# A two-layer transformer block in fp32 parts: the layer loop written out, its barrier removed, the last norm by sums per token

## The reference, cut to what matters

```python
for l in range(DEPTH):                      # DEPTH = 2, D_MODEL = 1024, SEQ = 512
    h = rmsnorm(x, norm_mix[l])
    proj = h @ w_in[l]                      # 1824 columns, split into the mixers' inputs
    ...                                     # convolution, two attentions, pooling
    x = x + jnp.concatenate([ya, yb, yc, yd], axis=-1) @ w_out[l]
    x = x + memory_cross_attention(rmsnorm(x, norm_xa[l]), mem, mem_norm[l], ...)
    x = x + conv_glu_ffn(rmsnorm(x, norm_ffn[l]), ffn_up[l], ffn_dw[l], ffn_dw_b[l], ffn_down[l])
return rmsnorm(x, norm_final)
```

## Time and profile before

| | before |
|---|---|
| median of 3 runs | 1663.12 us (1661.73 to 1664.53) |
| the profiled execution | 1663.39 us |
| its span, first to last instruction | 1661.4 us |
| TensorE busy | 1581.5 us, 95% |
| VectorE, ScalarE, GpSimd busy | 1037.2, 718.8, 188.4 us |
| mean granted TensorE clock | 0.983 of full |
| DMA | 153.44 MB, 92 GB/s, 28.4% of 16 engines on the main queue |

### The profile page before, as it was taken

How to read it: one execution, slowest core, us unless ns; L and a number is a source line. 1 busy time by engine, 2 the same in 40 slices (tenths; PEclk the granted TensorE clock), 3 DMA queues, 4 the chain that set the end, 5 groups by cost and what they waited for, 6 DMA issues and landing times. The chain is left out here.

```text
span 1661.4 us, 21870 instructions
## 1 busy us (share of the span) xinstructions
PE 1581.5 (95%) x7784; PEld 1230.0 (74%) x7784; DVE 1037.2 (62%) x1579; ACT 718.8 (43%) x1114; POOL 188.4 (11%) x133
## 2 busy tenths in 40 slices
PE   5699999999899999999979999999999999999995
PEld 1287677688688888888868767778768888888874
DVE  7659976543456746745756997654344773674676
ACT  8722477442435423423442257653244442342343
POOL 0005014230030000000020501422003000000002
PEclk9899999999999999999989999999999999999998
DMA  4242233132032323232224223312302323233223
GB/s 161 88 155 89 74 117 103 39 101 89 13 101 90 95 95 101 89 101 93 84 83 144 88 77 118 99 49 100 94 13 89 102 88 102 91 98 96 94 83 107
DMA packets 45441, 153.44 MB, mean 92 GB/s; under 512 B 5040, under 2 KB 5296, under 8 KB 44464
## 3 DMA queue, kind: packets, MB, share of 16 engines
q1 hardware_dynamic: 45360, 152.33, 28.4%
HBM read 144.97 MB, written 7.34 MB: 92 GB/s over the span
## 5 line engine op out<-in xcount | busy, mean ns | idle before, releaser
L705 ACT ACTIVATE wh<-raw 128x1024 fp32r<-128x1024 f32 x228 | 241.4, 1059 | 609.6 <-PE psum L1329 599.4
L1326 PE MATMUL psum<-a_hi,wh 128*128 128x512 f32 x1072 | 422.6, 394 | 3.7 <-DVE wl L978 3.7
L1329 PE MATMUL psum<-a_hi,wl 128*128 128x512 f32 x1072 | 419.9, 392 | 0.0
L1328 PE MATMUL psum<-a_lo,wh 128*128 128x512 f32 x1072 | 419.9, 392 | 0.0
L978 DVE TENSOR_TENSOR wl<-raw,wh 128x1024 fp32r<-128x1024 f32 x224 | 276.9, 1237 | 147.7 <-ACT wh L705 147.5
L1326 PE MATMUL psum<-b_hi,wh 128*128 128x512 f32 x608 | 241.1, 397 | 8.2 <-DVE x_sb L1210 4.4
L1326 PEld LDWEIGHTS psum<-a_hi,wh 128*128 128x128 f32 x1072 | 203.2, 190 | 46.2 <-DVE wl L978 4.3
L1328 PE MATMUL psum<-b_lo,wh 128*128 128x512 f32 x608 | 237.4, 390 | 0.0
L1329 PE MATMUL psum<-b_hi,wl 128*128 128x512 f32 x608 | 237.3, 390 | 0.0
L1329 PEld LDWEIGHTS psum<-a_hi,wl 128*128 128x128 f32 x1072 | 202.9, 189 | 42.8
L1328 PEld LDWEIGHTS psum<-a_lo,wh 128*128 128x128 f32 x1072 | 203.3, 190 | 41.9
(11 more groups left out here) (208 smaller groups left out, 1933.8 us busy)
## 6 DMA issues: line engine op xcount, KB each, us to landing
raw<-in_w_main SPq DMA_DIRECT2D x106, 512.0 KB, 3.5
raw<-in_w_up SPq DMA_DIRECT2D x88, 512.0 KB, 3.5
raw<-in_w_down SPq DMA_DIRECT2D x32, 512.0 KB, 3.5
raw<-in_w_last SPq DMA_DIRECT2D x16, 384.0 KB, 3.0
bias_scratch<-stage SPq DMA_DIRECT2D x16, 256.0 KB, 2.0
bias<-bias_scratch SPq DMA_DIRECT2D x16, 256.0 KB, 3.8
raw<-in_w_first SPq DMA_DIRECT2D x6, 512.0 KB, 3.5
sw<-in_small SPq DMA_DIRECT2D x2, 1152.0 KB, 8.2
```

The lines of the kernel that those rows point to most:

```text
L705: act.activation(wh[:, b].rearrange("p k m -> p (k m)")[:, 0:width], raw[:, b, 0:width], ACT.Copy).then_inc(w_hi, 1)
L1326: pe.matmul(out_ap, wh[:, b, k, :], his[:, k, :], start=((begin or first) and i == 0), stop=False)
L1328: pe.matmul(out_ap, wh[:, b, k, :], los[:, k, :], start=False, stop=False)
L1329: last = pe.matmul(out_ap, wl[:, b, k, :], his[:, k, :], start=False, stop=(end and i == len(tiles) - 1))
```

## The change

The loop over layers becomes Python code: a function layer_program(layer) returns five engine programs, which one single block runs one behind the other, layer 0 and then layer 1. Each layer has its own set of 59 semaphores; those that both share count on. There is no barrier and no clearing of semaphores between the layers or ahead of the last norm. Since 123 is odd, chunk n of layer 1 uses the other half and the other bank (function slot).

At the end of layer 0's feed-forward, ACT and VectorE split the first two weight chunks of layer 1 (hi_of_next, lo_of_next), where in earlier steps they split chunks n + 2. TensorE begins layer 1 with chunk 0, waiting for each tile of a_lo, then the sums, then chunk 1 with the row in its middle. SyncE issues the loads of the first two chunks of layer 1 under the same conditions as before, and the layer's vectors once all low parts of x are there.

In the last layer a_hi and a_lo are not made after the feed-forward. GpSimd sums the squares of 7 tiles, and TensorE takes the eighth straight from sqx: sixteen recorded one-column matmuls. The last norm is then done as the others, by a 128x4 corner and row_of, and the scalings read the row from PSUM. ACT runs a one-column square root (L971) ahead of the last eight chunks, which puts the table load there.

```diff
-        with nc.Fori(0, L) as layer:
-            with nc.Block() as block:
+        def layer_program(layer):
+            own, prev = layer_sems[layer], layer_sems[layer - 1] if layer else None
...
+            def slot(b):
+                return (b + layer * N_END) % 2
...
+                if prev:
+                    for b in range(2):
+                        sp.wait_ge(prev.w_lo, N_END - 1 + b)
+                        sp.dma_start(raw[:, slot(b), :], w_first[layer, b]).then_inc(w_load[b], 16)
+                    sp.wait_ge(prev.x_lo, 3 * KT)
                 sp.dma_start(vec[:], vecs[layer]).then_inc(vec_in, 16)
...
-                    for b in (1, 0):
-                        sp.wait_ge(w_lo, N_END - b)
-                        sp.dma_start(raw[:, b, :], w_first[layer + 1, b]).then_inc(w_load[b], 16)
-                    for b in range(2):
-                        sp.wait_ge(w_load[b], ((N_END + 1 - b) // 2) * 16)
...
+                if not prev:
                     hi(0)
                     hi(1)
                 roots("stat_mix", c("eps6"), 1.0 / D)
                 row_of("stat_mix")
                 hi(2)
...
+                if last_layer:
+                    act.activation(xneg[:, 0:1], c("ones"), ACT.Sqrt)
                 for i in range(KT):
                     n = N_END - KT + i
                     if i < KT - 2:
                         hi(n + 2)
+                    elif not last_layer:
+                        hi_of_next(i - KT + 2)
                     act.wait_ge(g_dve, g_dve_count(n, "down"))
-                    split_x(i, 2, v("g_next", i))
+                    split_x(i, 2, None if last_layer else v("g_next", i))
...
                 for i in range(KT):
                     n = N_END - KT + i
                     residual(i, n)
                     if i < KT - 2:
                         lo(n + 2)
+                    elif not last_layer and i == KT - 2:
+                        lo_of_next(0)
+                    if not last_layer:
                         split_x(i, 2, v("g_next", i))
+                if not last_layer:
+                    lo_of_next(1)
...
+                if prev:
+                    pe.wait_ge(prev.g_freed_by_dve, g_dve_count(N_END - 2, "down"))
+                    gemm(0, 0, a_hi, a_lo, ready=lambda i: pe.wait_ge(prev.x_lo, 2 * KT + i + 1))
+                    pe.wait_ge(prev.x_squares_summed, 3 * KT)
+                    sums_of("stat_mix", (ssum, one))
+                    pe.wait_ge(prev.g_freed_by_dve, g_dve_count(N_END - 1, "down"))
+                    gemm(1, 1, a_hi, a_lo, tiles=range(4), end=False)
+                    row_of("stat_mix")
+                    gemm(1, 1, a_hi, a_lo, tiles=range(4, KT), begin=False)
+                else:
                     sums_of("stat_mix", (ssum, one))
                     gemm(0, 0, a_hi, a_lo)
                     row_of("stat_mix")
                     gemm(1, 1, a_hi, a_lo)
...
-            nc.all_engine_barrier(sems_to_clear=all_sems)
+                if last_layer:
+                    pe.wait_ge(ss_in, 3 * KT - 1)
+                    pe.wait_ge(sq_in, 3 * KT)
+                    sums_of("stat_out", (ssum, one), (sqx[:, 1, :], one))
+                    row_of("stat_out")
...
-                pe.matmul(V[0], ones, ssum[:], start=True, stop=True).then_inc(v_full, 1)
...
+                act.activation(thin[:, OUT, 0:4], V[V_BANK["stat_out"]][:, 0:4], ACT.Sqrt, bias=c("eps6"),
+                               scale=1.0 / D).then_inc(of_last.root_of_stat, 1)
...
+                dve.reciprocal(thin[:, OUT, 0:4], thin[:, OUT, 0:4]).then_inc(of_last.root_inverted, 1)
+                dve.wait_ge(of_last.v_full, V_AT["stat_out_row"] + 1)
                 for k in range(KT):
-                    dve.scalar_tensor_tensor(x_sb[:, k, :], x_sb[:, k, :], v("g_next", k), rbc[:],
+                    dve.scalar_tensor_tensor(x_sb[:, k, :], x_sb[:, k, :], v("g_next", k), V[V_BANK["stat_out_row"]],
                                              ALU.mult, ALU.mult).then_inc(x_up, 1)
```

More of the change, by code:

```diff
@@ L13 @@
+from collections import namedtuple
 from contextlib import ExitStack
@@ new lines, in vector @@
+                PAIR_STEPS = 3
+                for g in range(GROUPS + 1):
+                    tiles, base, f0 = GROUP_TILES[g], N_UP + g * N_GROUP, g * GROUP
+                    up_pair(base, 0, f0, first=(g == 0), tail=False)
+                    before = step.n
+                    with dve.Fori(1, tiles) as j:
+                        step.enter((j - 1) * PAIR_STEPS + before)
+                        up_pair(j * 2 + base, j, j + f0)
+                        step.leave(PAIR_STEPS, tiles - 1)
+                    out_lo(tiles - 1, f0 + tiles - 1)
+                    if g < GROUPS:
+                        n = base + 2 * tiles
+                        for s in range(2):
+                            residual(s, n + s)
+                            lo(n + s + 2)
+                        with dve.Fori(1, KT // 2) as j:
+                            for s in range(2):
+                                residual(j * 2 + s, j * 2 + n + s, (N_UP + s) % 2)
+                                lo(j * 2 + n + s + 2, (N_UP + s) % 2)
@@ L1633, in block_program @@
[L1633 to L1654 removed]
+                gemms(0, 9, a_hi, a_lo, S, "in", lead=2)
@@ new lines, in tensor @@
+                for i in range(2):
+                    ps = bank(f"vm{i}")
+                    for t in range(2):
+                        kb = 2 * i + t
+                        last = pe.matmul(ps[:, GW * t:GW * t + GW], ckv[:, kb * P:kb * P + P], sw[:, SW_V:SW_V + GW],
+                                         start=True, stop=True)
+                    last.then_inc(v_full, 1)
+                gemm(12, 0, a_hi, a_lo, free="in")
+                gemm(13, 1, a_hi, a_lo, free="in")
+                gemm(14, 0, a_hi, a_lo, free="in", used=a_used)
@@ new lines, in tensor @@
+                gemm(N_OUT, 1, b_hi, b_lo, tiles=Y_TILES[7:], ready=y_ready, begin=False)
+                gemm(N_OUT + 1, 0, b_hi, b_lo, tiles=Y_TILES[7:], begin=False)
+                pe.wait_ge(half_lo, 1)
+                gemm(N_OUT + 2, 1, b_hi, b_lo, free="out", tiles=range(4), begin=False, end=False, first=True)
+                pe.wait_ge(w_lo, N_OUT + 3)
+                gemm(N_OUT + 2, 1, b_hi, b_lo, tiles=range(4, KT), begin=False)
+                gemms(N_OUT, KT, b_hi, b_lo, S, "out", lead=3)
@@ new lines, in norm_sum @@
+                def norm_sum(name, n):
+                    pe.wait_ge(ss_in, n)
+                    sums_of(name, (ssum, one))
+                gemm(N_WQ, 1, a_hi, a_lo, free="wq", ready=lambda i: pe.wait_ge(x_lo, i + 1))
+                norm_sum("stat_xa", KT)
+                gemm(N_WQ + 1, 0, a_hi, a_lo, free="wq", tiles=range(4), end=False)
+                row_of("stat_xa")
+                gemm(N_WQ + 1, 0, a_hi, a_lo, tiles=range(4, KT), begin=False)
+                gemms(N_WQ, KT, a_hi, a_lo, S, "wq", lead=2)
@@ L1656, in _ @@
+                if last_layer:
[3 more added lines that the diff above has]
+                    row_of("stat_out")
+            return sync, gpsimd, scalar, vector, tensor
+        layers = [layer_program(layer) for layer in range(L)]
+        of_last = layer_sems[L - 1]
+        OUT = ROOTS.index("stat_out")
+        with nc.Block() as block:
             @block.sync
@@ L1657, in _ @@
             def _(sp):
+                for sync, _, _, _, _ in layers:
+                    sync(sp)
                 for k in range(KT):
```

1886 lines of the change are left out of this document (924 added, 962 removed).

## The result

The changed kernel took 1647.24 us (median of four runs, 1644.67 to 1650.13), the kernel before 1663.82 in the same series: a ratio of 0.9898, 95% interval 0.9886 to 0.9910. The forecast was 1644.7 with a range of 1641 to 1650. The profiled execution took 1644.67 us, with a span of 1642.9 instead of 1661.4.

The account below looks back on a forecast made before the run. TensorE, busy 95% of the span, bounds the kernel; only the thin seam, end and layer 0 entry can pay. Gains 12.4 + 1.3 + 4.7 = 18.4 us off 1663.39 give 1645.0, less 0.27 for the median: 1644.7, range 1641 to 1650.

Parts of the forecast that it names:

- Seam: Between layer 0 and layer 1: last matmul to chunk 2 falls from 25.70 to 13.3 us, gain 12.4.
- The stall: At the old seam: TensorE follows GpSimd 3.2 us late, without instructions after the loop's jump back; gone in straight code.
- Rival (a): At the seam: TensorE stalls 3.2 us again on layer 1 code never run before, giving 1647.9 us; chance 0.10.
- Rival (d): TensorE's longer straight program: instructions come too slowly, stalls of 3.2 us each, ten make 1677 us; chance 0.04.
- Entry: Start of layer 0: a 1.28 us table load ahead of the first weight split goes with the loop; gain 1.3 us.
- End: Last residual to span's end: no barrier, per-token sums, smaller root and reciprocal; 14.4 instead of 19.1 us, gain 4.7.
- The row at twice 1.05: In the last norm: the row runs at the low clock, twice 1.05 us, less its overlap.
- Table load ahead of the last chunks: Ahead of layer 1's last eight chunks: ACT's 1.28 us square-root table load fits into 1.84 us idle, no cost.
- rival (b): Clock falls elsewhere: one short low stretch more or less, 1.7 us either way, 1643 or 1646.4; included in the forecast's 0.77.

Follow-up runs that it names:

- the run with two blocks: Changed kernel with an all-engine barrier and a second block put back between the layers, no hardware loop: 1653.13 us, ratio 0.9937.
- the fastest version: Changed kernel with two later TensorE waits taken away by order, and four VectorE convolution taps per layer moved to the attention's first steps: 1640.73 us, ratio 0.9860.

## Why the prediction was right, point by point

The profiled execution was forecast at 1645.0 and took 1644.67; each term can be held against it.

- **Seam:** forecast 13.3 us from the last matmul to chunk 2, measured 13.29. Its parts hold too: first chunk behind one pitch, sums at 5.44 us, a wait of 0.30 us for wl (forecast 0.35; the forecast's own terms, 2.85 less 2.60, make 0.25), 1.6 to 2.1 us to spare at tile 7 and at the sum (measured 2.06 and 1.57). Taking two rows of the kernel's own pattern inside a layer as the price of the seam was what made this exact.
- **The stall was the jump back's**, as assumed; the run with two blocks and the end of the kernel before show it. What the forecast had left out is that ScalarE was as late, with a table load of 1.28 us in front of its splits, and that chunk 0 waited for these. It changed nothing in the sum, since the forecast counted the seam as a whole. Rival (a) did not come: no "issue" idle stands at the seam.
- **Rival (d)** is refuted twice: from layer 0's last matmul to layer 1's it is 773.43 us, from the first chunk of layer 0 to that of layer 1 772.98, and the program without inner loops runs the same. The prediction's own evidence was misread: 769.0 and 770.0 are lengths of windows that were asked for. From the first chunk to the last matmul of a layer it was 773.96 and 772.67 us before, which says the same.
- **Entry:** forecast 1.3, measured 1.25 at the first matmul and 1.80 at the end of its chunk, since the clock rose at 84.6 instead of 87.0 and only seven matmuls instead of ten ran at the low one. Whether the longer fall at 136 (6.8 us instead of 3.4) has to do with the earlier start is not shown.
- **End:** forecast 14.4 us behind the residual, measured 14.7. The row at twice 1.05 was right in this execution (2.04). In the fastest version's profiled one it took 1.31, with the sums at full clock throughout, and the end 13.4 us. The scalings take from PSUM what they took from SBUF (5.35 and 5.39 us for eight). Within the term, what the prediction could not say is that 3.1 of the 4.4 us came from the missing barrier.
- **Table load ahead of the last chunks:** no cost, as the sum had it. By the 2.66 us that the Trainium skill, ScalarE: Activation LUTs, section What ACT_TABLE_LOAD costs, gives for a switch, the split would have been late; the trace shows 1.28 us and the next operation 0.01 us behind it, and measurement decides.
- **What was wrong:** rival (b), the clock, sized at 1.7 us either way for one short stretch. The stretches have no one price: behind the sums the first 3.4 us are free, since VectorE paces the stage, and 3.4 more cost 1.0; and stretches of 10 to 14 us among the products, which the rival did not have, make the stage 5 us longer (43.6 against 38.7 us). The forecast also carried the place of one execution (0.27 above the median of before) over to a kernel whose profiled execution was its fastest. Over the twelve runs of the changed kernel, its repetition and the one without inner loops the span rises 0.39 us for each us at the low clock (r 0.87; the clock is known to 0.001, which is 3.3 us of low time). The median's 2.5 us above the forecast fit that. They are more than the 1.7 us of rival (b): the range held the median by the room that it had for other terms, which were not needed, and that is luck.

What stays open is why the short fall behind the sums comes in one execution with 3.4 us and in another with 6.8 or not at all.

## What to carry to other kernels

Price a seam by the same pattern elsewhere in the trace, where it is not a seam: the two rows inside a layer gave it to 0.01 us (12.97, and 12.98 once nothing was late). Before an engine's idle time or a clock fall is taken away, look which engine paces that stage; TensorE made earlier there only waits later, and here a later wait of 2.4 us with its clock fall cost 5 us. Read the other engines' rows at a stall too: here ScalarE, not TensorE, held the first chunk of a layer. The cure was to shorten the queue ahead of the operation that frees PSUM, with work moved to where VectorE has room; it has a price, as TensorE then waits 1.30 us in each layer at the scores, a wait that was not there before.

## What the runs showed of the hardware

- At a wait of 2.4 to 2.6 us on TensorE among small products the clock fell to 1.2 GHz for 10.2 to 13.7 us in nine cases of nine; at waits of 1.0 us and less there in none of nineteen, two of them without an earlier fall behind the sums. At the output projection, waits of 2.2 us had a stretch of 3.4 us in 12 cases of 20.
- A jump back over a whole layer cost TensorE 3.2 us and ScalarE 3.4 us against GpSimd; entering new code behind a barrier cost TensorE 0.19 us and ScalarE nothing.
- ScalarE's table load takes 1.28 us and the next operation starts 0.01 to 0.02 us later, with no drain in sight on either side, where the next operation was ready.
- The layers begin at one of two distances from the span's start, whatever the edit: 79.1 to 79.6 us in nine profiled executions and 80.6 to 81.0 in five. The difference arises ahead of the layers, where no edit stands; it adds 1.0 to 1.9 us to the span and hides differences of that size between kernels.
